# Router and scan rearranged, held tiles moved to experts 18 to 24, and the second expert's weights requested tile by tile

## The reference, cut to what matters

```python
h = h + hybrid_mixer(rms_norm(h, norm1_g), ...)      # attention + scan, output projection w_out
tok = rms_norm(h, norm2_g)                           # 256 tokens x 1024
logits = tok @ w_router + b_router                   # 32 experts
top_v, top_i = lax.top_k(logits, 4); top_w = softmax(top_v)
for e in range(32):
    gate, up = split(tok @ w_gate_up[e] + b_gate_up[e])   # 1024 x 2048
    act = (clip(up) + 1) * (min(gate, 7) * sigmoid(1.702 * gate))
    out = out + dense_w[:, e:e+1] * (act @ w_down[e] + b_down[e])   # 1024 x 1024
h = rms_norm(h + out, final_g)
```

## Time and profile before

| | us |
|---|---|
| median of 3 runs | 1484.52 (1484.02 to 1488.02) |
| time of the profiled execution | 1488.63 |
| span of the profiled execution | 1486.8 |
| PE busy | 1389.7 (93%) |
| DVE busy / ACT busy | 373.8 (25%) / 225.0 (15%) |
| DMA, moved | 473.72 MB, mean 319 GB/s over the span |

### The profile page before, as it was taken

How to read it: one execution, slowest core, us unless ns; L and a number is a source line. 1 busy time by engine, 2 the same in 40 slices (tenths; PEclk the granted TensorE clock), 3 DMA queues, 4 the chain that set the end, 5 groups by cost and what they waited for, 6 DMA issues and landing times.

```text
span 1486.8 us, 14740 instructions
## 1 busy us (share of the span) xinstructions
PE 1389.7 (93%) x5960; PEld 582.4 (39%) x5960; DVE 373.8 (25%) x881; ACT 225.0 (15%) x456; POOL 48.0 (3%) x37
## 2 busy tenths in 40 slices
PE   7999989998999999999999999999999999999997
PEld 6874444444444443333333333333333333333332
DVE  5657762414310221211111121112111111211211
ACT  2114331023310020100100010001001000100101
POOL 1503110000000000000000000000000000000000
PEclk9999999999999989999999999999999999999998
DMA  9453232072337547999999999999999999999993
GB/s 366 159 188 124 86 114 85 1 292 104 114 116 294 205 170 334 428 436 425 435 431 430 436 424 436 429 431 435 427 436 426 435 433 428 436 424 434 419 387 131
DMA packets 23232, 473.72 MB, mean 319 GB/s; under 512 B 3776, under 2 KB 3936, under 8 KB 5376
## 3 DMA queue, kind: packets, MB, share of 16 engines
q1 hardware_dynamic: 23152, 473.24, 75.9%
q10 hardware_dynamic: 48, 0.03, 0.0%
HBM read 472.18 MB, written 1.08 MB: 318 GB/s over the span
## 4 chain that ended last, share of the span: by engine, by line
PE 60%; DMA 31%; DVE 5%; ACT 2%; issue 1%; POOL 0%; SPq 0%; DVEq 0%; ACTq 0%; POOLq 0%
DMA weights<-in_w_gate_up_dram 31%; PE ps L934 20%; PE ps L640 7%; PE ps L538 6%; PE ps L958 5%; PE ps L720 4%; PE ps L728 4%; PE ps L563 2%; PE ps L512 2%; PE ps L833 2%; PE ps L811 2%; DVE arena L1338 2%; PE ps L968 1%; PE ps L572 1%; ACT hnT L1023 1%
## 5 line engine op out<-in xcount | busy, mean ns | idle before, releaser
L934 PE MATMUL ps<-weights,hnT 128*64 128x512 f32 x2000 | 440.5, 595 | 21.6 <-DMA weights<-in_w_gate_up_dram 21.6
L934 PEld LDWEIGHTS ps<-weights,hnT 128*64 128x64 f32 x2000 | 139.3, 137 | 318.2 <-issue 277.3
L958 PE MATMUL ps<-weights,hnT 128*64 128x512 f32 x1016 | 226.8, 599 | 7.7 <-ACT hnT L1023 7.7
L1023 ACT ACTIVATE hnT<-ps 128x512 f32<-128x512 f32 (+1 forms) x96 | 50.5, 526 | 806.0 <-PE ps L512 574.0
L1614 DVE TENSOR_SCALAR ssmT<-ps 128x512 f32<-128x512 f32 x32 | 22.1, 692 | 525.8 <-PE ps L934 525.8
L958 PEld LDWEIGHTS ps<-weights,hnT 128*64 128x64 f32 x1016 | 70.5, 137 | 143.9 <-issue 128.1
L640 PE MATMUL ps<-weights,hnT 128*128 128x512 f32 x224 | 98.0, 594 | 1.6 <-issue 1.6
L538 PE MATMUL ps<-hnT,weights 128*128 128x272 f32 x352 | 81.4, 393 | 0.0
L538 PEld LDWEIGHTS ps<-hnT,weights 128*128 128x128 f32 x352 | 66.7, 190 | 14.0 <-issue 0.4
L968 PE MATMUL ps<-hnT 64*128 64x512 f32 x256 | 63.6, 615 | 8.8 <-ACT hnT L1023 8.8
L512 PE MATMUL ps<-const,ssmT 128*128 128x128 f32 x320 | 49.2, 284 | 22.1 <-DVE ssmT L1621 21.4
(11 more groups left out here) (211 smaller groups left out, 938.1 us busy)
## 6 DMA issues: line engine op xcount, KB each, us to landing
weights<-in_w_gate_up_dram SPq DMA_DIRECT2D x57, 4096.0 KB, 20.2
weights<-in_w_down_dram SPq DMA_DIRECT2D x30, 4096.0 KB, 20.1
weights<-in_w_blocks_dram SPq DMA_DIRECT2D x28, 2048.0 KB, 8.1
weights<-in_w_gate_up_dram SPq DMA_DIRECT2D x4, 3072.0 KB, 12.3
weights<-in_w_gate_up_dram SPq DMA_DIRECT2D x5, 2048.0 KB, 7.2
arena<-in_w_gate_up_dram SPq DMA_DIRECT2D x5, 1024.0 KB, 12.8
weights<-in_w_down_dram SPq DMA_DIRECT2D x2, 2048.0 KB, 9.0
weights<-in_w_down_dram SPq DMA_DIRECT2D x1, 3072.0 KB, 12.1
```

The lines of the kernel that those rows point to most:

```text
L934: mm = pe.matmul(bank(4 + b)[64 * a:64 * a + 64, :], xe[:, 2 * (k % 4) + k // 4, :], w[:, FF * b + 512 * a:FF * b + 512 * a + 512], start= ...
L958: mm = pe.matmul(bank(7)[64 * c:64 * c + 64, :], actT[:, P * j + SLOTS * a:P * j + SLOTS * a + SLOTS], pair[kk % 2][:, 512 * c:512 * c + 5 ...
L1023: return nc.scalar.activation(o, i, ACT.Copy)
```

## The change

It has seven parts.

1. **Scan**: the two row tiles of each group are transposed into banks 4 and 5, and wait for ACT's copies of the group before (`xrow_ok`) instead of `y_read`.
2. **Router**: the last `out_proj` is split in halves with transposes and router matmuls between them; `routed` comes straight from the one-hot table, before the weights; `hn2` is made by ACT; all of `open_sums` comes before the positions; the gather comes before the counts.
3. **Expert 1** is loaded in six gate-up pieces (four of 1 MiB, two of 2 MiB) and four down pieces of 1 MiB, each after the same tiles of expert 0. The loop of loads starts at expert 2.
4. **Held tiles** now belong to experts 18 to 24, one each (six gate-up, one down). Experts 18 to 31 are straight code.
5. **Scatter** of an expert comes after the gate-up of the next.
6. **Down biases** are added in experts 12 and 13, half in each. PE gets filler matmuls (`keep_warm`): one before expert 0, three in the last expert.
7. **Last expert**: the last gate-up part and the down part are loaded in two halves each, and DVE copies the last `y_sb`.

```diff
-HELD = {27: [("gu", 0), ("gu", 1)], 28: [("gu", 0)], 29: [("gu", 0)], 30: [("gu", 0), ("dn", 3)], 31: [("gu", 0)]}
+FINE = EXPERTS - 1
+BIASED = 12
+HELD = {18: [("gu", 0)], 19: [("gu", 0)], 20: [("gu", 0)], 21: [("gu", 0)], 22: [("dn", 3)], 23: [("gu", 0)], 24: [("gu", 0)]}
...
+FIRST_TILES = ((0, 1), (1, 2), (2, 3), (3, 4), (4, 6), (6, 8))
...
-                        sp.wait_ge(freed, (u - ago) * counts + counts // parts * (i + 1))
                         width = 2 * SLOT // per
-                        load(e, i, slice(width * (need[0] - per * i), width * (need[-1] + 1 - per * i)))
+                        halves = [need[:len(need) // 2], need[len(need) // 2:]] if peeled and u == FINE and i == parts - 1 else [need]
+                        for n, part in enumerate(halves):
+                            sp.wait_ge(freed, (u - ago) * counts + counts * (part[-1] + 1) // KD)
+                            load(e, i, slice(width * (part[0] - per * i), width * (part[-1] + 1 - per * i)), late_half[kind] if n else None)
...
-            with sp.Fori(1, LOOPED) as u:
+            for first, last in FIRST_TILES:
+                sp.wait_ge(gu_free, last)
+                load_gate_up(1, first // 4, slice(FF * 2 * (first % 4), FF * 2 * ((last - 1) % 4 + 1)))
+            for i in range(4):
+                sp.wait_ge(dn_free, i + 1)
+                load_down(1, 0, slice(2 * D * i, 2 * D * i + 2 * D))
+            with sp.Fori(2, LOOPED) as u:
```

```diff
-                    pe.wait_ge(y_read, 2 * g)
+                    pe.wait_ge(xrow_ok, 3 * g)
                 for t in range(RT):
                     for j in range(4):
-                        mm = turn(bank(t)[:, P * j:P * j + P], xbcT[:, 4 * g + j, real(t)])
+                        mm = turn(bank(4 + t)[:, P * j:P * j + P], xbcT[:, 4 * g + j, real(t)])
...
-            def out_proj(t, c):
+            def out_proj(t, c, ks=range(KD)):
                 loaded(pe, f"WO{c}")
                 pe.wait_ge(uT_act, t + 1)
                 pe.wait_ge(uT_dve, t + 1)
-                for k in range(KD):
+                for k in ks:
                     mm = pe.matmul(bank(2 * t + c), uT[:, k, P * t:P * t + P], wslot(f"WO{c}")[:, k, :],
...
-            def turn_rows(t):
-
-                pe.wait_ge(h2_ok, 2 * t + 2)
-                for k in range(KD):
-                    mm = turn(bank(4 + 2 * t + k // 4)[:, P * (k % 4):P * (k % 4) + P], hrow[:, t, P * k:P * k + P])
+                if ks[-1] == KD - 1:
+                    mm.then_inc(wo_ps, 1)
+
+            def turn_rows(t, cs):
+
+                pe.wait_ge(h2_ok, 2 * t + cs[-1] + 1)
+                for c in cs:
+                    for i in range(4):
+                        k = 4 * c + i
+                        mm = turn(bank(4 + 2 * t + c)[:, P * i:P * i + P], hrow[:, t, P * k:P * k + P])
...
+            def router(t, c):
+                if c == 0:
+                    pe.wait_ge(h2T_dve, t + 1)
+                else:
+                    pe.wait_ge(h2T_act, t + 1)
+                for k in range(4 * c, 4 * c + 4):
                     mm = pe.matmul(bank(4 + 2 * t)[:, 0:EXPERTS], hn2T[:, k, P * t:P * t + P], w_r[:, k, :],
                                    start=(k == 0), stop=(k == KD - 1))
-                mm.then_inc(logit_ps, 1)
+                if c:
+                    mm.then_inc(logit_ps, 1)
...
-            turn_rows(0)
-            out_proj(1, 1)
+            turn_rows(0, (0, 1))
+            out_proj(1, 1, range(4))
+            turn_rows(1, (0,))
             pe.wait_ge(wr_ok, 1)
-            router(0)
-            turn_rows(1)
-            router(1)
-
-            def open_sums(t):
-
-                for c in range(2):
-                    mm = pe.matmul(bank(2 * t + c), ident, hrow[:, t, 512 * c:512 * c + 512], start=True, stop=False, skip_group_check=True)
-                return mm
-
-            open_sums(0)
-            pe.wait_ge(dense_ok, 1)
-
+            router(0, 0)
+            router(0, 1)
+            out_proj(1, 1, range(4, KD))
+            router(1, 0)
+            turn_rows(1, (1,))
+            open_sum(0, 0)
+            router(1, 1)
+            open_sum(0, 1)
+            open_sum(1, 0)
+            open_sum(1, 1).then_inc(scat_ps, 1)
+
+            pe.wait_ge(routed_ok, 1)
...
-            for t in range(RT):
-                mm = pe.matmul(bank(4)[:, 0:32], ones, routed[:, t, :], start=(t == 0), stop=(t == 1))
-            for t in range(RT):
-                mm = turn(bank(7)[0:EXPERTS, P * t:P * t + P], dense_w[:, t, :])
-            mm.then_inc(route_ps, 1)
-            open_sums(1).then_inc(scat_ps, 1)
+            def counts():
+
+                for t in range(RT):
+                    pe.matmul(bank(4)[:, 0:32], ones, routed[:, t, :], start=(t == 0), stop=(t == 1))
+                pe.wait_ge(dense_ok, 1)
+                for t in range(RT):
+                    mm = turn(bank(7)[0:EXPERTS, P * t:P * t + P], dense_w[:, t, :])
+                mm.then_inc(route_ps, 1)
+
+            def keep_warm(n, width=512):
+
+                for i in range(n):
+                    pe.matmul(bank(6)[:, 0:width], ident, cst("slots")[:, 0:width], start=True, stop=True)
```

```diff
-            def unit(u, ahead, peeled=False):
+            def unit(u, ahead, peeled=False, owed=True, biases=()):
                 gate_up(u, peeled)
+                if owed:
+                    scatter(u)
+                down_bias(biases)
                 turn_selection(u)
                 if ahead:
                     gather(u + 1)
-                elif isinstance(u, int):
-                    down_bias(range(3))
+                else:
+                    keep_warm(2)
                 turn_act(u)
                 if ahead:
                     turn_tokens(u + 1)
-                elif isinstance(u, int):
-                    down_bias(range(3, 4))
+                else:
+                    keep_warm(1, P)
                 down(u, peeled)
                 if ahead:
                     start_bias(u + 1)
-                scatter(u)
-
+
+            gather(0)
+            counts()
+            turn_tokens(0)
+            pe.wait_ge(xrow_sb, 1)
+            keep_warm(1)
             pe.wait_ge(bias_part, 6)
             pe.wait_ge(count_ok, 1)
+            start_bias(0)
             pe.wait_ge(dwT_ok, 1)
-            prepare(0)
-            with pe.Fori(0, LOOPED) as u:
+            unit(0, True, owed=False)
+            with pe.Fori(1, BIASED) as u:
+                unit(u, True)
+            unit(BIASED, True, biases=range(2))
+            unit(BIASED + 1, True, biases=range(2, 4))
+            with pe.Fori(BIASED + 2, LOOPED) as u:
                 unit(u, True)
             for u in range(LOOPED, EXPERTS):
                 unit(u, u < EXPERTS - 1, peeled=True)
+            scatter(EXPERTS)
             over = pe.value_load(n_over[0:1, 0:1], min_val=0, max_val=OVERFLOW_MAX)
             with pe.If(over > 0):
                 with pe.Fori(0, over) as j:
                     prepare(j + EXPERTS)
-                    unit(j + EXPERTS, False, peeled=True)
+                    unit(j + EXPERTS, False, peeled=True, owed=False)
+                    scatter(j + EXPERTS + 1)
         @block.scalar
         def _(act_e):
```

```diff
+            act_e.wait_ge(rstd2, 3)
+            act_f(hn2[:, 0, :], hrow[:, 0, :], ACT.Copy, scale=rstat[:, 6:7]).then_inc(hn2_ok, 1)
             act_e.wait_ge(negv_ok, 1)
             for t in range(RT):
                 i = act_f(e4[:, t, 0:4], v8[:, t, 0:4], ACT.Exp, bias=rstat[:, 8 + t:9 + t], accum_out=rstat[:, 10 + t:11 + t])
             i.then_inc(e4_ok, 1)
+            act_f(hn2[:, 1, :], hrow[:, 1, :], ACT.Copy, scale=rstat[:, 7:8]).then_inc(hn2_ok, 1)
             act_f(stat[:, 12:13], stat[:, 8:9], ACT.Sigmoid)
...
+            V.tensor_reduce(routed, pick.rearrange("p t (i e) -> p t e i", i=TOP_K), AX.X, ALU.add).then_inc(routed_ok, 1)
             dve.wait_ge(e4_ok, 1)
             link(V.reciprocal(rstat[:, 10:12], rstat[:, 10:12]))
             link(V.tensor_tensor(w4[:, :, 0:4], e4[:, :, 0:4], rstat[:, 10:12].unsqueeze(2).broadcast_to([P, 2, 4]), ALU.mult))
+            dve.wait_ge(routed_ok, 1)
             link(V.tensor_tensor(pick4, pick4, w4[:, :, 0:TOP_K].unsqueeze(3).broadcast_to([P, 2, TOP_K, EXPERTS]), ALU.mult))
-            link(V.tensor_reduce(dense_w, pick.rearrange("p t (i e) -> p t e i", i=TOP_K), AX.X, ALU.add))
-            V.tensor_scalar(routed, dense_w, 0.0, None, ALU.is_gt).then_inc(dense_ok, 1)
-            for t in range(RT):
-                V.tensor_scalar(hn2[:, t, :], hrow[:, t, :], rstat[:, 6 + t:7 + t], None, ALU.mult).then_inc(hn2_ok, 1)
-
+            V.tensor_reduce(dense_w, pick.rearrange("p t (i e) -> p t e i", i=TOP_K), AX.X, ALU.add).then_inc(dense_ok, 1)
...
+            dve.wait_ge(dn_free, EXPERTS * 4)
+            V.tensor_copy(y_sb, bank(7)).then_inc(ysb_ok, 1)
```

51 lines of the change are left out of this document (28 added, 23 removed).

## The result

The changed kernel takes 1475.06 us (median of 4 runs, 1474.33 to 1478.17), the kernel before beside it 1484.63 us (1484.02 to 1488.02): ratio 0.9914, 95% interval 0.9894 to 0.9934. The difference of the medians is 9.6 us where 20.1 were forecast. These two medians have a ratio of 0.9936, just outside that interval, so four runs each leave the size uncertain: by the ratio the gain is 12.8 us, and in a second measurement further down 12.7 us (1475.73 against 1488.40). In the following the medians are used. The profiled execution took 1478.17 us, 3.1 above its median, with a span of 1476.1.

A forecast was written before the change was run, and what follows sets the result against it. Bound: full DMA weight stream, 29.17 us per expert, then PE from expert 27. Last gate-up landing 1462.4 less 17.0 (held), 3.4 (pieces), 2.5 (router), scan 0, gives span 1466.7, 20.1 less; 1484.5 - 20.1 = 1464.4 us, range 1457 to 1475.

The forecast's parts named there:

- rival B: Straight experts: PE needs 28.3 us instead of 27.2, losing about 7 to 9 of the 17 us: 1473; chance 0.15.
- Scan, taken as 0: Scan's transposes: PE starts 1.5 us earlier but waits 1.5 us more before `y_diag`; 0, bounds 0 and -4.5 us.
- rival C: Front of the kernel: scan waits vanish (-4.5) and router's clock stays up (another -2.4): 1457.5 with both; chance 0.14.
- Router, -2.5: Last `out_proj` to expert 0: gather could start at 548 to 550 instead of 552.81; -2.5 us, bounds -4.9 and +1.
- with the clock full: Router case with PE's clock not at half: expert 0 starts 4.9 us earlier, against about 1.1 at half clock.
- Expert 0 at 553 to 557: Sign that the prediction is right: expert 0 starts at 553 to 557 us, where it started at 557.76.
- Pieces, request at 33.0 us: Expert 1's loads: expert 2 requested 33.0 us after expert 0's start, not 36.4; -3.4 us, bounds -1.2 and -5.3.
- Expert by PE, 27.2 us: Expert loop with scatter after gate-up: PE needs 27.2 us per expert instead of 27.91; bounds 26.7 and 27.9.
- Held tiles, 17.0 us of stream: Experts 18 to 24: seven held tiles at 2.43 us each shorten the weight stream by 17.0 us.
- the model of the prediction: Weight stream: request plus 2.2 us latency plus 19.45 us for eight tiles, then 29.17 us per expert.
- Rival A: Expert loop: PE's clock falls in waits of about 2.0 us, 32.4 us per expert, about 1550 us; chance 0.04.
- The end: Expert 31: gate-up ends at 1444.7, down starts 5.6 us later, takes 7.1, ends at 1457.4; span ends at 1466.7.

## Why the prediction was right, and where it was not

The direction held (faster by over 0.3%), but only about half of the forecast gain came (9.6 us of 20.1), and 1475.06 us lies on the upper end of the range (1475), 10.7 above the number. That it still lies there is luck in part: the range reached up to 1475 for the sake of rival B, which did not come true, and the losses that did come had no place in it. Against the span of 1466.7 the profile shows 1476.1, 9.4 more. By the prediction's own steps:

- **Scan, taken as 0 with bounds 0 and -4.5: the step that failed.** Where PE's time goes was right to the hundredth (13.93 us before, after, and with fillers), and rival C's -4.5 is refuted. The bounds were wrong: they left no room for a loss. The sentence "PE starts 1.5 us earlier and waits 1.5 us more before `y_diag`" says where the idle time goes, and I did not ask what stands around it there. It costs 6.3 to 6.4 us by the two pairs of medians, which would be about 60% of the miss; 3.6 to 4.9 us by the traces of the groups 1 to 3; and 1.6 to 3.1 us by the ratios of the other sets.
- **Router, -2.5 (-4.9 to +1):** -4.8 in the profiles, the lower bound (-3.2 by the medians, within the intervals). What I called "with the clock full" is what happened. Counted from `out_proj`, the positions start 0.9 us earlier (29.9 us behind it, 30.8 before), the gather follows them after 2.5 us instead of 6.1, as the opening matmuls are out of the way, and expert 0 follows the gather after 4.7 instead of 5.0. The first bound stood nearer than the middle that I took.
- **Expert 0 at 553 to 557:** 560.81 (+7.9 up to `out_proj`, of which 3.7 in the groups where the edit acts; router -4.8). With the scan as before it starts at 552.45 to 553.65 in the four profiles of it whose scan kept its clock and whose router is new.
- **Pieces, request at 33.0 us:** 32.8. The gain of 3.4 us was 2.85 by the pair of profiles and 2.1 by the medians.
- **Expert by PE, 27.2 us (26.7 to 27.9):** 26.69. Down starts 5.5 us after gate-up; down has no wait at 605.69. Rival B, a PE too slow for the held experts, is refuted: they keep the DMA share at 1.00, and PE's periods are 26.7 to 26.9 us (1074.65, 1101.40, 1128.16, 1155.02). Expert 22 alone takes 29.3 us (1181.92 to 1211.26): only a down tile of it is held, and PE waits 2.43 us for its gate-up. "Near 27 for 18 to 24" did not allow for that.
- **Held tiles, 17.0 us of stream:** the stream carried that much less, but came late. By the model of the prediction, from expert 2's request: 593.60 + 2.2 + 19.45 + 28 x 29.17 - 17.0 = 1415.0, and PE's wait in expert 30 ends at 1418.86. The model was 0.6 us early before, too; 3.3 us are new. From the halves above: 907.80 to 967.26 is 1.1 us over two periods of 29.17 (the experts 12 and 13, the first straight ones, and the two that add the down biases), and 1054.77 to 1272.78, eight periods with the seven tiles, is 218.0 against 216.4. **That step too was mis-sized; its cause is open.** No run was made for it. The stretch from 1060 to 1300 moves 430 GB/s against 432, which alone would be 1.1 us. Two other traces narrow it down. With the scan as before in the third set there is no loss from expert 12 to 15 (900.69 to 988.18, 87.49 us for three periods of 29.17), and yet as much by expert 26 (1295.22, 3.2 us late by the model; 2.8 in the changed kernel), so straight code or biases have no fixed price. With the held tiles at 27 to 31 the stream loses 0.7 us from expert 12 to 25 (905.40 to 1285.29, 379.89 us for 379.21), where the changed kernel loses 2.8; so most of it goes with the held tiles at 18 to 24, or with the straight code of the experts 18 to 26, which moved with them.
- **Rival A, the clock falls in the waits.** Its mechanism is real: behind waits of 2.25 to 2.36 us seven halves run 1.6 to 1.7 us slow. Its price is not: 1.6 us is below the 2.0 us of slack from which I let it decide, so the stream hides it in every expert but one. In expert 30, where PE ends last, it lies on the path. A rival that I had priced at 87 us was worth at most 1.6 in the loop; the run with fillers there showed no gain in the total. I had put the mechanism only where the long waits are and not in the scan.
- **The end:** gate-up of 31 at 1444.7; it came at 1454.19. (At the forecast landing PE is 1.8 us past the end of the first half, not short of it as the prediction's words have it; the 5.2 us that it then takes are those of a PE that is past it.) From the wait's end in expert 30 (forecast 1410.3) the sum is: first expert +5.5, request -0.2, stream +3.3, clock in expert 30 +1.6, faster PE -0.7, together +9.5. Gate-up's end to down 5.5 us (5.6), down 7.09 (7.1), its end to the span's end 9.3 (9.3): right to a tenth each.

The worths of the single parts (3.3 for the held tiles, 3.2 for the router, 2.1 for the pieces, 1.4 for the scatter, all by medians and all with intervals that overlap) do not add up to the whole, and needn't: parts share the same slack of PE and the same stream. The end's part was not tested by itself; the profiles give it the 8.78 - 7.09 = 1.7 us of the last down.

## What to carry to other kernels

When a wait is removed from a chain whose end is set by another engine, follow the idle time to its new place and look at what stands around it. Here it came to lie in two gaps beside short matmuls, and PE's clock fell for a cost of up to 6 us where the edit had no gain to give; a filler matmul in each gap, or the old order, gave most of it back. That the idle time in these two places does it is shown by the fillers; that the short matmuls beside it count, and not the two gaps alone, is not tested. Price such an edit with a bound on the losing side too, and check every stretch's granted clock after a change, not the engine's share alone: PE was busy longer (1405.0 us against 1389.7), mostly because it was slower.

## What the runs showed of the hardware that I had not expected

- In the scan two gaps of about 1 us, one shortly behind the other among short matmuls, were followed by a fall of the granted clock in all four profiles with the new order, while the gap of 1.51 us before transposes with 0.36 us behind it left it at 1.00 in six of seven. The total idle time was nearly the same (2.05 against 1.87 us). In group 0, with one wait of 0.97 us, the clock fell in three of these eleven profiles. The Trainium skill (TensorE: Matmul & The Clock Gate, HAM oscillation) describes a kernel that loses the clock by waiting for data between tiles. The trace agrees that the clock can fall behind waits, but here they are of about 1 us in the scan and 2.25 in the loop, shorter than those of the page's example.
- In an expert loop with PE busy 96% of the time (814.15 of 850 us) waits of 2.25 us were followed by a half at 7.09 us (703.64) or at 8.7 to 8.8 (732.81). Waits of about 1.0 us, in the run with the late scatter and in the kernel before, were followed by none that was slow; in the former the clock is 1.00 over 880 us.
- The times of one and the same kernel mostly follow its mean clock: in one set the kernel before took 1483.97 us at 0.996 and 1493.05 us at 0.987 (in another, one of 1487.91 at 0.996 does not fit). So part of the spread between executions goes with the clock, and with the scan's fillers the spread was 2.9 us, against 6.5 in the same set, over six executions each.
- What stays open: why the stream of weights lost 3.3 us on the way, most of it only where the held tiles belong to experts 18 to 24 and straight code begins there. The fetches of code grew from 0.36 to 0.57 MB, which is a sign at most.
